# Down weights of the experts loaded from ScalarE's queue instead of SyncE's

## The reference

```
def moe(x, router_w, router_b, w_gate, w_up, w_down):
    ...   # each token picks 2 of 16 experts; comb holds their weights
    hid = jax.nn.silu(jnp.einsum('bld,edf->blef', x, w_gate)) * jnp.einsum('bld,edf->blef', x, w_up)
    hid = hid * comb[..., None].astype(hid.dtype)
    return jnp.einsum('blef,efd->bld', hid, w_down)
```

## Time and profile before

| | us |
|---|---|
| median of 3 runs | 1201.53 |
| lowest and highest of them | 1195.73 and 1302.72 |
| the profiled execution | 1200.29 |
| its span, first to last instruction | 1198.6 |
| PE busy | 930.8 (78%) |
| DVE busy | 412.2 (34%) |
| POOL busy | 283.4 (24%) |
| ACT busy | 186.0 (16%) |
| mean granted clock of PE, as a share of full speed | 0.822 |

### The profile page before, as it was taken

One profiled execution on the slowest core, in us unless ns is written; L12 is line 12 of the kernel. 1 busy time (PEld: TensorE's weight loads), 2 busy tenths in 40 slices (PEclk: granted clock), 3 DMA queues, 4 the chain that ended last, 5 costly groups with the idle time before them and its releaser, 6 DMA issues.

```text
span 1198.6 us, 11197 instructions
## 1 busy us (share of the span) xinstructions
PE 930.8 (78%) x4366; PEld 544.5 (45%) x4366; DVE 412.2 (34%) x805; ACT 186.0 (16%) x313; POOL 283.4 (24%) x434
## 2 busy tenths in 40 slices
PE   7999979988795497878788539999544987777870
PEld 5888769865342233333333429954212333332320
DVE  4897043634224321112231167611353111111116
ACT  1311301110202111100111241210221111000111
POOL 3699921402015121111211110000111211111110
PEclk9999967985597699888899665579855988888895
DMA  9456390124007499999999733320362999999953
GB/s 239 146 187 241 142 315 2 31 59 135 14 7 295 174 376 407 415 408 410 407 418 371 288 80 106 108 67 10 155 232 92 383 410 415 406 411 408 418 217 143
DMA packets 77509, 286.09 MB, mean 239 GB/s; under 512 B 25881, under 2 KB 44775, under 8 KB 62454
## 3 DMA queue, kind: packets, MB, share of 16 engines
q1 hardware_dynamic: 63242, 256.25, 55.6%
q10 hardware_dynamic: 9092, 20.42, 5.1%
q0 software_dynamic: 5120, 8.66, 2.2%
HBM read 265.82 MB, written 26.40 MB: 244 GB/s over the span
## 4 chain that ended last, share of the span: by engine, by line
PE 74%; DVE 10%; issue 8%; DMA 4%; ACT 2%; POOL 0%; POOLq 0%; ACTq 0%; SPq 0%; DVEq 0%
PE ps L1568 20%; PE ps L316 10%; PE ps L1587 9%; PE ps L2152 5%; PE ps L1550 3%; PE ps L840 2%; PE ps L2016 2%; PE ps L2031 2%; DMA ring<-s_out_mats 2%; PE ps L555 1%; PE ps L819 1%; PE ps L1332 1%; DVE work L1287 1%; DVE work L1779 1%; PE ps L568 1%
## 5 line engine op out<-in xcount | busy, mean ns | idle before, releaser
L1568 PE MATMUL ps<-ring,work 128*64 128x512 f32 x512 | 257.0, 660 | 75.1 <-issue 73.8
L1569 PE MATMUL ps<-ring,work 128*64 128x512 f32 x512 | 257.5, 661 | 0.0
L1568 PEld LDWEIGHTS ps<-ring,work 128*64 128x64 f32 x512 | 74.9, 152 | 221.9 <-issue 219.7
L1608 DVE TENSOR_TENSOR work<-ps,work 64x512 f32<-64x512 f32 x32 | 34.1, 1067 | 327.7 <-ACT work L1597 327.7
L1587 PE MATMUL ps<-ring,work 128*64 128x512 f32 x256 | 116.6, 598 | 1.4 <-DVE work L1613 1.4
L1588 PE MATMUL ps<-ring,work 128*64 128x512 f32 x256 | 116.6, 598 | 0.0
L316 PE MATMUL ps<-work,ring 128*128 128x264 f32 x512 | 115.2, 387 | 0.0
L316 PEld LDWEIGHTS ps<-work,ring 128*128 128x128 f32 x512 | 96.8, 190 | 16.4
L1111 POOL TENSOR_TENSOR ring<-ring 128x512 f32<-128x512 f32 (+5 forms) x76 | 90.5, 1208 | 9.0 <-DVE ring L1107 5.7
L1569 PEld LDWEIGHTS ps<-ring,work 128*64 128x64 f32 x512 | 74.9, 152 | 0.0
L1630 POOL COPY work<-work 64x1 int32<-64x1 int32 x32 | 5.7, 178 | 287.1 <-PE ps L1550 244.2
(11 more groups left out here) (453 smaller groups left out, 1316.1 us busy)
## 6 DMA issues: line engine op xcount, KB each, us to landing
ring<-in_moe_w_gate SPq DMA_DIRECT2D x32, 2048.0 KB, 16.9
ring<-in_moe_w_up SPq DMA_DIRECT2D x32, 2048.0 KB, 23.1
ring<-in_moe_w_down SPq DMA_DIRECT2D x32, 2048.0 KB, 24.4
ring<-in_w_in ACTq DMA_DIRECT2D x6, 2048.0 KB, 8.6
s_out_mats<-ring SPq DMA_DIRECT2D x4, 1280.0 KB, 4.7
ring<-s_out_mats SPq DMA_DIRECT2D x1, 5120.0 KB, 22.9
ring<-in_w_in SPq DMA_DIRECT2D x2, 2048.0 KB, 10.4
s_in_mats<-ring SPq DMA_DIRECT2D x4, 1024.0 KB, 6.3
```

Of the source, the lines that this page charges most:

```text
L1568: nc.tensor.matmul(ps[0:SLOT, 2 + s, :], xgT[s][:, c], gate_w[s][:, c], start=c == 0, stop=c == DC - 1)
L1569: last = nc.tensor.matmul(ps[SLOT:P, 2 + s, :], xgT[s][:, c], up_w[s][:, c], start=c == 0, stop=c == DC - 1)
L1608: nc.vector.tensor_tensor(hid[s][0:SLOT].rearrange("t (c p) -> t p c", c=4), strided(ps[SLOT:P, 2 + s, :]), strided(sg[s][SLOT:P]), ALU.mu ...
```

## The change

`down_load` is called for the experts 2 to 15 from ACT, in `moe_act`, behind `act_y` of expert k-1 and for expert k+1, and no longer from SP. SP's program keeps the down loads of the experts 0 and 1 and all gate/up loads. The waits of `down_load` and the slots are the same. `at_expert_load` gives the arguments that `down_load` takes.

```diff
@@ -1651,6 +1651,10 @@
             return k, k // 2, k % 2
 
+        def at_expert_load(k):
+
+            return k, k, k // 2, k % 2
+
         def further_rounds(eng, tag, body):
@@ -1716,6 +1720,8 @@
                     act_tokens(a, l, *at_expert(k + 1))
                 if k > 0:
                     act_y(a, l, *at_expert(k - 1))
+                    if k + 1 < NE:
+                        down_load(a, l, *at_expert_load(k + 1))
             act_y(a, l, *at_expert(NE - 1))
@@ -1748,9 +1754,6 @@
             down_load(q, l, 1, 1, 0, 1)
             for k in range(2, NE):
                 gate_up_load(q, l, k, k, k // 2, k % 2)
-                if k > 2:
-                    down_load(q, l, k - 1, k - 1, (k - 1) // 2, (k - 1) % 2)
-            down_load(q, l, NE - 1, NE - 1, (NE - 1) // 2, (NE - 1) % 2)
```

## The result

The changed kernel takes 1211.14 us (median of 4 runs, 1206.81 to 1212.23) against 1200.43 of before beside it, a difference of 10.7 us. One of before's four runs took 1302.72 us in a slower state; without it before's median is 1199.33 us and the difference 11.8. The ratio without that run is 1.0096, 95% interval 1.0052 to 1.0139: the change is slower by 1%, where 1212 was forecast. The profiled execution has a span of 1210.5 us, 11.9 more than before's.

What follows compares the result with a forecast made beforehand. The 16 DMA engines were taken to bound both expert stages, at about 410 GB/s. Stage 0's 5.4 + 0.7 = 6.1 us and stage 1's 5.4 sum to 11.5 on 1200.29, so 1212 us, range 1200 to 1224.

Steps and rivals of the forecast that it cites:

- The step that carries it: Both expert stages: one down transfer moves ahead of every gate/up; the last product starts 5.4 us later in each stage.
- The share: DMA engines with two loaded queues: ACT's queue gets 39% of the bytes, read from the y rows behind stage 0.
- start-up of 1.6 us: Down loads on ACT's queue: about 1.6 us of start-up, added to 13.1 us of transfer at 0.39.
- Down of 15 behind Bm: End of stage 0: down of 15 shares the engines with Bm and lands late, costing 0 to 3.6 us, 0.7 taken.
- that case: End of stage 0: at an exact half for each queue, down of 15 costs nothing and the sum is 10.8 us.
- The tail: Stage end, from the last gate/up start to ACT's last copy: all PE's own work, stays at 15.5 us.
- The rate: DMA in both expert stages, some 430 us: stays at 410 GB/s with two queues, no change counted.
- rival E: ACT: the moved issues only block it, 14 us, giving 1226; counted under D, 0.13 together.
- the prediction's signs: Both stages: down loads land 13 to 16 us after issue, up loads after over 23.6, last products start 5 to 6 later.
- Rivals B: DMA queues: the loads keep their order, so nothing moves and the time is 1200 to 1201 us; chance 0.16.
- C: DMA engines: two queues keep them fuller, 426 GB/s, so the kernel is faster at 1196 us; chance 0.09.
- D: Two queues cost rate, or down of 15 starves: 1223 us at 400 GB/s, 1253 at 374; 0.13 with rival E.

Runs made afterwards that it cites:

- the two kernels that issue late: Before with each down load of k on SP ahead of gate/up of k+1, 1228.76 us; the change with down loads 2 to 14 behind their own silu, 1216.54 us.
- the first run: Against before: all loads on SP, but each down load of k ahead of gate/up of k+1 and not behind it; 1228.76 us, ratio 1.0231.

## Why the prediction was right

**The step that carries it** was: one down transfer, 5.1 us, moves ahead of every gate/up, and at the end that isn't given back. The last product starts 231.4 to 232.4 us into a stage in the four stages with all loads in SP's old order that I lay side by side (before, and the unchanged stages of the two one-stage runs), and 236.1 to 237.4 in the eight stages of the change, its repeat, the one-stage runs and the run with 14 alone. The means are 231.9 and 236.9, 4.9 apart. The one other run in the old order with no work added on PE, the one with the load of 1 earlier, has 233.1 and 231.6. That one load suffices is shown by the run with 14 alone, where up of 15 lands 4.9 us later after an unmoved issue. That its return takes the lateness away is shown in part only: with the last two back, 4.2 and 2.1 us of it are left.

**The share** of 0.39 came from two unequal queues at another place and was too small. While both queues carried bytes, the load of 14 had a half of them. The start-up of 1.6 us was too short: q10 had no packet for 3.4 us behind the issue. The forecast gave the load 1.6 + 13.1 = 14.7 us from issue to landing; it was through by 640, 13.6 us after its issue. That these two errors nearly cancel is luck, but the step doesn't rest on it: there was room for 19.5 us. The Trainium skill's rule of turns between queues ("DMA: Bandwidth & Descriptors", "Queues, rings and completion order") is borne out while both are loaded: in 538:544 of the changed kernel q1 moved 1.26 MB in 85 packets and q10 1.25 in 80. Another rule of the Trainium skill, on the same page, that several issuing engines save only sequencer time ("Issuing engines are not separate DMA queues"), would have left the time at 1200.3 and was the poorer guide: the engines are the same, but who is served first is not.

**Down of 15 behind Bm** was given 0.7 us of 0 to 3.6 and cost nothing. Its 2.10 MB were through by 657, about where the forecast had them at a share of one half (656.0), and PE had no wait for it. The prediction had named that case, with 10.8 us as its sum.

**The tail** behind the last gate/up start was to stay at 15.5 us. It did in stage 0 and was 18.1 in stage 1. This is a term that the sum lacked: a stall may leave PE at the low clock for its last product. Before, the stalls of over 3 us fall on the experts 4, 6 and so on to 14, and the products behind them take 8.5 to 10.1 us, all others but the first 7.1; 15 is one without. In stage 1 of the change the first of them is at expert 3, and from there they fall on the odd experts, 15 among them (3.7 us). The low clock in the last product cost 0 and 2.6 us in the two stages of the change, 1.7 and 0 in its repeat, and it doesn't come from the change alone, as the 10.0 us in an unchanged stage show. Against it stood 1.3 us of a shorter last scatter, which the sum lacked too. Between the two profiled executions the terms are 4.5 and 5.5 us of later starts (5.4 each in the forecast), 2.6 of low clock, 1.3 less for the scatter, and 0.6 by which stage 0 began later, ahead of the change: 11.9, for a sum of 11.5. The main term is right and carries the result; that the total came so close is luck, since the small ones happen to cancel.

**The rate** was taken as unchanged, 410. It is 405 in the change. Leaving out the two kernels that issue late (383, and 392 with 384), it is 401 to 407 in every stage with many loads on both queues, against 409 to 411 in those with SP alone or one load on ACT, but for one of 407, where the 20 extra matmuls held PE up. The 35 windows of 10 us over 385 GB/s average 411 in the change, as the 38 of before do (409 in the repeat), so under load the engines are hardly slower. What differs are dry spells, such as this one:

```profile
550.00:560.00 10.00, 7.65 (x22) 2.54 (x24) 0.00 (x0) 0.00 (x0) 0.00 (x0) 0.59 1.00 426
560.00:570.00 10.00, 10.00 (x56) 3.96 (x54) 3.38 (x6) 1.75 (x3) 2.63 (x6) 1.00 0.79 301
```

PE had stalled 8.9 us for gate/up of 9, its product ended at 562.3, and only then could gate/up of 11 be issued. As gate and up come later, their slots come free later, and the line of loads gets thinner. The loads' order thus has a second effect, of which the first run is the extreme case. How many microseconds of the result it is isn't settled: the start of the last product is 5 us late with it (the change) and without it (14 alone), so at the end it seems hidden. In the run with the last two back the last products are 4.2 and 2.1 us late from what happened up to expert 13, where both effects are at work; no run parts them, nor in the 6 us of the run with up on ACT.

**ACT.** The issues took 0.33 us each, not 0.5, and beside the copy. ACT's result copies wait 98.6 us for PE in both kernels, and rival E fell with that. Its wait ahead of the silu grew from 329.6 to 342.3 us, as the gate/up products end later. Of the prediction's signs, the down loads land 16.1 us after their issue (median; 24.4 before), just at the edge of the 13 to 16. The starts are 4.5 and 5.5 us late for 5 to 6. One sign was wrong: an up load was to land later than 23.6 after its issue, and that of 15 needs 22.9. Its issue had moved with the slot, 5.3 us later into the stage; with 14 alone the issue stays and the sign holds (28.5).

**Two readings** of the prediction are a little off and change nothing. The rate of its slices is 406 to 418 GB/s but for the two at the edges of the stages, 371 in slice 21 and 383 in slice 31. And its 12.8 us for an expert without a stall hold 0.74 us of waiting; PE's own pace is 11.9 to 12.0.

Rivals B (the order stays) and C (more rate) fell, the one by the 2.10 MB, the other by the 405 GB/s. D had the right sign on the rate, 1.2%, at a small part of its price.

## What to carry to other kernels

Where transfers bound a stage, a second queue isn't free: it lets what is issued later and needed later pass what is waited for, and the price is one such transfer at the end of each stage, where nothing behind it hides it. Keep the urgent and the patient load in one queue in the order of need: a queue that held the urgent loads alone, as SP's did after the change, didn't protect them. Moving only the load that passes the last product's weights shows in one run whether that is enough for the cost. And look at the depth of the line before an issue is delayed for the sake of order: with two slots for each weight, 4.4 us later on each gate/up cost 29 us.

## What the runs showed of the hardware

While q1 and q10 both had transfers of 2 MB, they moved the same bytes (1.26 and 1.25 MB in 6 us), beside 0.12 MB of POOL's queue. The load of 14, issued on ACT's queue at 626.42 while SP's was full, had no packet until 629.8, and was through by 640. The last gate/up product of a stage (16 pairs of matmul records) took 7.1 us at a granted clock of 1.00 throughout and up to 10.0 us where it began at the low one. Stalls of nearly the same length came out differently: 3.0 us was followed by a product of 10.0 us in the unchanged stage 0 of one run, 8.8 in stage 0 of the repeat and 7.1 in stage 0 of the run with that stage alone, so the length of the stall alone doesn't say it.
